# Unscaled u leaves PSUM on ScalarE, with q's first tile ahead of the token factors of x, and a scan ahead of a weight split

## What is computed

```python
hn = rms_norm(h, norm_mix[l])
proj = hn @ w_in[l]
u_ssm = proj[..., :D_SSM]                       # 512 channels, to the S5 mixer
q = rms_norm(proj[..., 512:1024] ..., attn_qn)  # 8 heads of 64
k = rms_norm(proj[..., 1024:1536] ..., attn_kn)
v = proj[..., 1536:]
y_ssm = s5_mixer(u_ssm, ...)                    # a diagonal linear recurrence over the tokens, gelu, a gate
y_att = moba_attention(q, k, v, rel_bias)
h = h + concat([rms_norm(y_ssm, ...), rms_norm(y_att, ...)]) @ w_out[l]
h = h + memory_cross_attention(rms_norm(h, ...), rms_norm(mem, ...), ...)
h = h + conv_ffn(rms_norm(h, ...), ...)
```

## Time and profile before

| | us |
|---|---|
| median of 3 runs | 671.12 (670.17 to 671.66) |
| the profiled execution's own time | 670.81 |
| its span | 668.8 |
| TensorE busy in it | 656.2 |
| VectorE busy | 487.2 |
| ScalarE busy | 340.6 |
| GpSimd busy | 172.5 |

### The profile page before, as it was taken

How to read it: one execution, slowest core, us unless ns; L and a number is a source line. 1 busy time by engine, 2 the same in 40 slices (tenths; PEclk the granted TensorE clock), 3 DMA queues, 4 the chain that set the end, 5 groups by cost and what they waited for, 6 DMA issues and landing times.

```text
span 668.8 us, 10548 instructions
## 1 busy us (share of the span) xinstructions
PE 656.2 (98%) x3914; PEld 542.1 (81%) x3914; DVE 487.2 (73%) x801; ACT 340.6 (51%) x587; POOL 172.5 (26%) x177
## 2 busy tenths in 40 slices
PE   8899999999999999999999999999999999999997
PEld 7688778877888788887998888888888888888886
DVE  5998998578766665557697666666656687868967
ACT  6538564766745464764354333334334345554662
POOL 4998992223220102330000111011110121100000
PEclk9999999999999999999999999999999999999999
DMA  8868515666120404030357555564566446655663
GB/s 296 309 206 130 167 44 145 177 185 221 64 66 1 158 2 188 4 124 0 127 189 249 199 182 188 192 225 151 186 222 218 151 170 223 211 189 140 182 196 125
DMA packets 67737, 106.99 MB, mean 160 GB/s; under 512 B 15792, under 2 KB 40496, under 8 KB 66288
## 3 DMA queue, kind: packets, MB, share of 16 engines
q1 hardware_dynamic: 64528, 100.17, 45.9%
q10 hardware_dynamic: 3168, 6.29, 2.9%
HBM read 89.54 MB, written 15.73 MB: 157 GB/s over the span
## 4 chain that ended last, share of the span: by engine, by line
PE 80%; DVE 11%; ACT 3%; SPq 2%; DMA 2%; issue 1%; POOL 1%; ACTq 0%; DVEq 0%
PE pb L510 23%; PE pb L512 23%; PE pb L511 23%; PE pb L1962 6%; PE pb L1965 4%; DVE F L1384 3%; DVE wring L500 2%; ACT F L993 1%; DMA raw<-in_w_in 1%; SPq L664 1%; DMA F<-scr_y 1%; DVE F L1390 1%; DVE pb L1384 1%; DVE sq L1432 1%; DVE wring L1384 1%
## 5 line engine op out<-in xcount | busy, mean ns | idle before, releaser
L510 PE MATMUL pb<-xs,wring 128*128 128x512 f32 (+1 forms) x400 | 149.6, 374 | 0.7 <-POOL xs L911 0.7
L512 PE MATMUL pb<-xs,wring 128*128 128x512 f32 (+1 forms) x400 | 148.9, 372 | 0.0
L511 PE MATMUL pb<-xs,wring 128*128 128x512 f32 (+1 forms) x400 | 148.9, 372 | 0.0
L1390 DVE SCALAR_TENSOR_TENSOR F<-pb,cols,F 128x511 f32<-128x511 f32 x88 | 65.9, 748 | 71.6 <-ACT F L993 69.7
L500 DVE TENSOR_TENSOR wring<-raw,wring 128x1024 fp32r<-128x1024 f32 x70 | 93.4, 1336 | 8.0 <-ACT wring L489 7.9
L510 PE MATMUL pb<-wring,xs 128*128 128x512 f32 x240 | 98.5, 411 | 0.3 <-DVE wring L503 0.3
L993 ACT ACTIVATE F<-pb,cols 128x512 f32<-128x512 f32 x50 | 38.2, 767 | 115.3 <-PE pb L512 115.2
L512 PE MATMUL pb<-wring,xs 128*128 128x512 f32 x240 | 93.9, 391 | 0.0
L511 PE MATMUL pb<-wring,xs 128*128 128x512 f32 x240 | 93.7, 390 | 0.0
L510 PEld LDWEIGHTS pb<-xs,wring 128*128 128x128 f32 x400 | 75.3, 188 | 14.1 <-issue 1.3
L512 PEld LDWEIGHTS pb<-xs,wring 128*128 128x128 f32 x400 | 75.3, 188 | 13.2
(11 more groups left out here) (152 smaller groups left out, 1011.1 us busy)
## 6 DMA issues: line engine op xcount, KB each, us to landing
raw<-in_ffn_w_up SPq DMA_DIRECT2D x22, 1024.0 KB, 5.3
F<-in_ffn_w_down SPq DMA_DIRECT2D x11, 1024.0 KB, 4.9
scr_w<-F SPq DMA_DIRECT2D x11, 1024.0 KB, 3.9
F<-in_x SPq DMA_DIRECT2D x8, 512.0 KB, 8.6
raw<-in_w_in ACTq DMA_DIRECT2D x4, 1024.0 KB, 6.3
raw<-in_w_out SPq DMA_DIRECT2D x4, 1024.0 KB, 4.9
raw<-scr_w SPq DMA_DIRECT2D x8, 512.0 KB, 3.8
raw<-scr_w SPq DMA_DIRECT2D x15, 256.0 KB, 4.7
```

Source lines behind the costliest of these rows:

```text
L510: nc.tensor.matmul(ps, lh, rh, start=first, stop=False)
L511: nc.tensor.matmul(ps, lh, rl_, start=False, stop=False)
L512: return nc.tensor.matmul(ps, ll, rh, start=False, stop=last)
L1390: return V.scalar_tensor_tensor(out=o, in0=a, scalar=s1, in1=b, op0=o1, op1=o2)
```

## The change

ScalarE now copies u0 to u3 out of PSUM, unscaled and reordered by step, into `uT` ahead of its copy of the factors. VectorE scales `uT` in place by `xbc` (`u_scale`): tile 0, then `turns(1)`, then tiles 1 to 3. A new semaphore `u_ready` counts the scaled tiles; SP's `u_write(q)` waits for it, and so does ScalarE ahead of `rows("q", qk)`, which overwrites `xbc`. On TensorE the factors of x are transposed after q's first tile (unit 4, t = 0) instead of between u1 and the last products of u2. On VectorE `scan(1)` moves ahead of the low part of unit 11.

```diff
--- before.py
+++ after.py
@@ -211,6 +211,7 @@
 
         raw_in = [sem("raw_in0"), sem("raw_in1")]
         piece_in = [sem(f"piece_in{i}") for i in range(len(PIECES))]
+        u_ready = sem("u_ready")
         k_hi, u_hi, u_lo, x0_in = sem("k_hi"), sem("u_hi"), sem("u_lo"), sem("x0_in")
         x_in = [sem(f"x_in{t}") for t in range(TT)]
         mem_in, memt_in = sem("mem_in"), sem("memt_in")
@@ -642,7 +643,7 @@
                 sync.dma_start(memr[:, t, :], A["mem"][0, t * 128:(t + 1) * 128, :]).then_inc(mem_in, 16)
 
             def u_write(q):
-                after_drain(sync, f"u{q}")
+                sync.wait_ge(u_ready, q + 1)
                 sync.dma_start(scr_u[q * 128:(q + 1) * 128].rearrange("p i k -> p (i k)"), uT[:, q, :])\
                     .then_inc(su_out if q else su0_out, 16)
 
@@ -1039,6 +1040,8 @@
             split_hi(act, U_Q + 1)
             by_step = lambda a: a.rearrange("p (k i) -> p i k", i=L)
             steps_first = lambda a: a.rearrange("p (i k) -> p i k", i=L)
+            for m in range(4):
+                drained(A_(steps_first(uT[:, m, :]), by_step(read(act, f"u{m}")[:, :]), ACT.Copy), f"u{m}")
             drained(A_(steps_first(xbc), by_step(read(act, "xb")[:, :]), ACT.Copy), "xb")
             split_hi(act, U_Q + 2)
             act.wait_ge(mem_in, 16 * MT)
@@ -1115,7 +1118,7 @@
             kernels_in(0)
             load_chunk(act, 5)
             split_hi(act, 9)
-            after_drain(act, "u3")
+            act.wait_ge(u_ready, 4)
             rows("q", qk)
             split_hi(act, 10)
             inv_root("q")
@@ -1537,18 +1540,17 @@
             root("x", xr_ready)
             split_lo(dve, U_Q)
 
-            def u_evac(m):
-
-                by_step = lambda a: a.rearrange("p (k i) -> p i k", i=L)
-                steps_first = lambda a: a.rearrange("p (i k) -> p i k", i=L)
-                p = read(dve, f"u{m}")
+            def u_scale(m):
+
+                after_drain(dve, f"u{m}")
                 if m == 0:
                     after_drain(dve, "xb")
-                drained(tt(steps_first(uT[:, m, :]), by_step(p[:, :]), steps_first(xbc), ALU.mult), f"u{m}")
-
-            for m in range(4):
-                u_evac(m)
+                tt(uT[:, m, :], uT[:, m, :], xbc, ALU.mult).then_inc(u_ready, 1)
+
+            u_scale(0)
             turns(1)
+            for m in range(1, 4):
+                u_scale(m)
             split_lo(dve, U_Q + 1)
             split_lo(dve, U_Q + 2)
             turns(2)
@@ -1614,8 +1616,8 @@
             head_event("q", qk, range(TT), H, "q")
             split_lo(dve, 10)
             head_rows("q", qk, range(TT), H, HD)
+            scan(1)
             split_lo(dve, 11)
-            scan(1)
             split_lo(dve, 12)
             dve.wait_ge(gain_in, 16)
             b = COL["ssm_b_glu"]
@@ -2037,13 +2039,14 @@
                             last = u_pass(m, k, a)
                         if k == KD - 1:
                             filled(last, f"u{m}")
-                            if m == 1:
-                                pe.wait_ge(xr_ready, 1)
-                                token_factors("xb", "x")
                 if k0 + n in (2, 4, 6):
                     last.then_inc(unit_used, 1)
 
-            proj(4, U_Q, "q")
+            for t in range(TT):
+                proj_tile(4, U_Q, "q", t)
+                if t == 0:
+                    pe.wait_ge(xr_ready, 1)
+                    token_factors("xb", "x")
             def weights_in(q):
 
                 pe.wait_ge(w1p_ready, q + 1)
```

## The result

| | before | after |
|---|---|---|
| median of 4 runs each, us | 670.88 (670.17 to 671.66) | 680.61 (679.12 to 681.09) |
| ratio, 95% interval | | 1.0141, 1.0121 to 1.0161 |
| profiled execution's own time, its span, us | 670.81, 668.8 | 680.3, 678.5 |

By the ratio the kernel became 9.4 us slower (8.1 to 10.8); the medians differ by 9.7. The forecast was 9.4 and 680.5. But how the sum came about differs from what I wrote: its first half was larger, and of the second 1.6 us of wait are left.

What follows compares the result with a forecast made beforehand. TensorE, busy 656.2 of 668.8 us, bounds the kernel. outputs(1) starts 8.5 us later, the clock adds 1.3, later waits return 0.4: +9.4, 680.5 on the median of 671.12; range 675.0 to 684.5.

Steps and rivals of the forecast that it cites:

- its first half: Up to proj(5): unit 5's low part late, +5.5, and the clock's fall, 1.3; TensorE 6.8 us late.
- the second: scan(1) ahead of unit 11's low part: TensorE waits 2.6 us ahead of qt2, plus 1.3 for the clock.
- renamed, not removed: At q's first tile: the 2.57 us wait for the factors becomes 2.3 for unit 4's low part, behind the same root.
- ScalarE's hold on qt2: Load of chunk 7 waits for unit 11's low part; qt_evac(0), queued behind it, frees qt2's bank only at 89.5.
- The step of proj(5): Unit 5's low part done at 45.5, so proj(5) starts then instead of at 40.09: +5.5 us.
- The price of 1.42 for a product: VectorE's u scaling: each SBUF-only 128x512 product takes 1.42 us while GpSimd works, 0.62 when it is idle.
- The clock's fall at proj(5): Half clock behind TensorE's wait at proj(5) adds 1.3 us, making TensorE 6.8 late.
- The step at qt2: TensorE arrives by 86.9, waits 2.6 us for ScalarE's evacuation ending at 89.5; clock's fall then adds 1.3.
- rival (a): Only the first loss counts, TensorE at least 9.5 us late at proj(5): +5.9, 677.0 us; chance 0.12.
- q's mean: VectorE's head_rows("q"): mean at about 68.5 instead of 64.39, VectorE 4.1 us late; bounds 2 and 6.5.
- qt2 to outputs(1), the old waits gone: TensorE from qt2 to outputs(1): 3.8 us of work with no wait; the old 0.92 wait goes.
- behind outputs(1): TensorE's smaller later waits, each under 0.9 us, give back perhaps 0.4 us.

Runs made afterwards that it cites:

- the last form: Kernel before, with only scan(1) ahead of unit 11's low part and ScalarE's load of chunk 7 behind the four qt_evac: 669.13 us, ratio 0.9984.
- the first half alone: Changed kernel with scan(1) put back behind unit 11's low part, all else of the change kept: 679.13 us, ratio 1.0128 to the kernel before.
- chunk 7 loaded late: Whole changed kernel with ScalarE's load of chunk 7 moved behind the four qt_evac: 678.28 us, ratio 1.0119 to the kernel before.
- the factors at their old place: The first half alone, with TensorE's transposes of x's factors back between u1 and the rest of u2, scaling still in SBUF: 677.72 us, ratio 1.0122.
- GpSimd paused: The first half alone, with GpSimd made to wait for u_ready 4 ahead of ca_table(0): 674.07 us, ratio 1.0063 to the kernel before.
- root early: Kernel before, only u0 copied unscaled, scan(1) moved, chunk 7 loaded late, turns(0) behind u's scalings, unit 6's low part ahead of turns(1): 670.45 us, ratio 1.0008.

## Why the prediction was right, and where it was not

**Right:** the direction, and its mechanism. The wait for the root of x was renamed, not removed: 3.01 us ahead of q's first tile, forecast 2.3. TensorE had no slack against unit 5's low part: it started proj(5) 0.06 to 0.07 us after that part was done, in both kernels, and in the last form it gained nothing there from a first tile of q that began 1.0 us earlier. The SBUF products were slow by GpSimd. ScalarE's hold on qt2 exists: the scan's move with it is 6.6 us slower than before, and 7.6 slower than without it. The write of u0, ScalarE's copies of u and the new wait ahead of q's rows cost nothing, as forecast: the timeline of the changed kernel shows no wait at them.

**The step of proj(5) was too small**: +5.5 forecast, +8.4 measured. By its own terms: VectorE starts again at 37.48, not 35.55 (0.35 of the 1.93 is an execution that was later from the start, its root at 30.80 and not 30.45, the rest is the half clock behind the first wait, which I had put at the high end only); `u_scale(0)` and `turns(1)` took 4.70, not 4.06; the other three products 5.06, not 4.26; the low part 1.21, not 1.65. The price of 1.42 for a product came from four at another place; here three of the four took 1.53 to 1.88. Why they are dearer here than there stays open; GpSimd was busy at both places.

**The clock's fall at proj(5) was too cheap**: 1.3 forecast, 1.8 measured. I had read it off ten operations behind a wait of 2.59. It has no single price. The 24 products of proj(5) took 7.93 us in the first half alone, 8.30 with chunk 7 loaded late, 7.97 with the factors at their old place and 7.21 with GpSimd paused, against 5.60 before: 1.6 to 2.7 lost, behind waits of 2.55 to 7.74, and about 2.5 behind the wait of 5.20 ahead of qt2. At the place of the first wait the half clock lasted until about 34.3 behind 2.59 us of wait, until about 38.8 behind 3.01 in the changed kernel, and did not come at all behind 3.16 in the run with the factors at their old place (granted clock 1.00 from 31.2 to 34.5) or behind 2.32 in the last form. So one execution's row gives the size of one fall and not a price to add elsewhere.

**The step at qt2 was too large**: a wait of 2.6 with half clock forecast, 1.58 at full clock measured. TensorE would have reached qt2 9.7 us late, not 6.8, and ScalarE's evacuation ended at 91.3, not 89.5. It is my rival (a), half-way: its condition, a TensorE at least 9.5 us late, was met, and still a wait was left, because the evacuation was later too. Its 1.8 us are the 1.31 for which `scan(1)` waited for TensorE's states (it started at 82.01, not 80.7) and a low part of some 2.1 us, not 1.7. That VectorE was ready for the scan at 80.7, just as forecast, is chance: q's mean came at 72.13, 7.7 us late and not 4.1, and the four products of q's rows then took 3.47 us and not the 5.67 of the earlier trace rows.

**The total is right in part by luck.** In the order of the forecast's own terms:

| term, us | forecast | measured |
|---|---|---|
| proj(5) starts later | 5.5 | 8.4 |
| half clock behind it | 1.3 | 1.8 |
| from there to qt2 | 0 | -0.5 |
| wait ahead of qt2 | 2.6 | 1.6 |
| half clock behind that wait | 1.3 | 0 |
| qt2 to outputs(1), the old waits gone | -0.9 | -1.0 |
| behind outputs(1) | -0.4 | -0.6 |
| sum | 9.4 | 9.7 |

The first two terms were 3.4 us too small, the next three 2.8 too large. A part of this offset follows from the mechanism: the later TensorE comes, the less is left of the wait at qt2. The rest does not: that the evacuation came 1.8 us later than forecast and that the clock did not fall again, which I had priced at 1.3, nearly cancel, and no run ties the one to the other.

## What to carry to other kernels

Ask of a wait that is to be filled with other work what that work waits for: q's first tile needed the same VectorE queue, one operation further on, and every operation behind the new wait on VectorE came later by it. Moving an operand from PSUM to SBUF changes with whom a VectorE product collides, not only its own length. A DMA issued from a compute engine's queue, behind a semaphore, is a barrier for the evacuations behind it; look for such an issue before a producer of that semaphore is moved.

## What the runs showed of the hardware

The product of 128x512 with both inputs in SBUF took 0.6 us beside an idle GpSimd and up to 1.9 beside a busy one; I had taken 1.42 for the price beside a busy one. GpSimd's table ended at 46.8 after the change, 3.2 us earlier than the 49.98 of the earlier trace rows, although VectorE's products were in its way. Beside a VectorE that was idle for most of their time, GpSimd's two operations of 256 columns took 1.5 us instead of 2.8. Its five operations of 576 columns took 8.8 us instead of 11.0 beside a busy VectorE, three of whose operations there were of 512 columns, where all were of 1024 before; whether that is why, no run shows. The granted clock fell to 0.50 around some waits of TensorE of 1.9 us (root early) to 7.7 us and stayed at 1.00 around others of 1.5 to 3.2 us, among them two at the place where it fell around the kernel before's 2.59.
